# Modulation products of a transformer program as streamed TensorE matmuls in four column strips

## The reference

```python
cond = jax.nn.silu(c)
for l in range(DEPTH):
    mod = cond @ ada_w[l] + ada_b[l]          # [1024] @ [1024, 6144], DEPTH = 2
    sh1, sc1, g1, sh2, sc2, g2 = [m[:, None, :] for m in jnp.split(mod, 6, axis=-1)]
    h = _rms_norm(x, norm_mix[l]) * (1.0 + sc1) + sh1
    y = _even_mixer(h, ...) if l % 2 == 0 else _odd_mixer(h, ...)
    x = x + g1 * (y @ w_out[l])
    h = _rms_norm(x, norm_ffn[l]) * (1.0 + sc2) + sh2
    x = x + g2 * _swiglu(h, ffn_gate[l], ffn_up[l], ffn_down[l])
```

## Time and profile before

| | |
|---|---|
| median of three runs | 3065.33 us (3062.31 to 3065.77) |
| the profiled execution | 3062.31 us; its span is 3062.3 us, nothing lies around it |
| busy: PE, DVE, ACT, POOL | 91%, 46%, 35%, 35% of the span |
| mean granted TensorE clock | 0.918 of full speed |
| loads | 264.5 MB, DMA engines 27% busy |

### The profile page before, as it was taken

One profiled execution on the slowest core, in us unless ns is written; L12 is line 12 of the kernel. 1 busy time (PEld: TensorE's weight loads), 2 busy tenths in 40 slices (PEclk: granted clock), 3 DMA queues, 4 the chain that ended last, 5 costly groups with the idle time before them and its releaser, 6 DMA issues.

```text
span 3062.3 us, 34663 instructions
## 1 busy us (share of the span) xinstructions
PE 2800.6 (91%) x12655; PEld 2262.4 (74%) x12655; DVE 1417.1 (46%) x2167; ACT 1071.9 (35%) x1745; POOL 1077.0 (35%) x535
## 2 busy tenths in 40 slices
PE   4985689999999988999999999999999999799998
PEld 3764357777787667888878888888888765588886
DVE  6489872455412784222123566523331279533312
ACT  2221432322323474333223555523332322433321
POOL 1321000344443223444423565544444321144442
PEclk6897656999999999999988999999999999899998
DMA  7431040355433101223221221123322221122231
GB/s 215 138 110 55 1 138 14 97 164 164 137 100 85 63 28 56 83 82 110 94 74 55 69 69 56 56 83 100 105 91 92 86 63 41 42 96 96 96 97 55
DMA packets 277694, 264.50 MB, mean 86 GB/s; under 512 B 23020, under 2 KB 276557, under 8 KB 277581
## 3 DMA queue, kind: packets, MB, share of 16 engines
q1 hardware_dynamic: 277581, 262.97, 27.0%
HBM read 260.85 MB, written 2.10 MB: 86 GB/s over the span
## 4 chain that ended last, share of the span: by engine, by line
PE 71%; DVE 14%; issue 7%; DMA 3%; ACT 2%; POOL 2%; SPq 1%; DVEq 0%; ACTq 0%; POOLq 0%
PE bank L1151 17%; PE bank L1153 16%; PE bank L1152 16%; DMA root<-in_ada_w_dram 2%; DVE ada_acc L2392 2%; POOL w_lo L809 2%; PE bank L1099 1%; PE bank L883 1%; PE bank L885 1%; PE bank L884 1%; DVE bank L2216 1%; PE bank L1509 1%; DVE root L2398 1%; PE bank L1440 1%; DVE score L2575 1%
## 5 line engine op out<-in xcount | busy, mean ns | idle before, releaser
L809 POOL TENSOR_TENSOR w_lo<-w_raw,w_hi 128x1024 fp32r<-128x1024 f32 (+1 forms) x364 | 865.6, 2387 | 1674.2 <-ACT w_hi L1758 1103.3
L1151 PE MATMUL bank<-h_hi,w_hi 128*128 128x512 f32 x1632 | 651.6, 399 | 25.8 <-DVE h_lo L2359 11.6
L1152 PE MATMUL bank<-h_lo,w_hi 128*128 128x512 f32 x1632 | 645.4, 395 | 0.0
L1153 PE MATMUL bank<-h_hi,w_lo 128*128 128x512 f32 x1632 | 644.6, 395 | 0.0
L1758 ACT ACTIVATE w_hi<-w_raw 128x1024 fp32r<-128x1024 f32 (+1 forms) x232 | 232.2, 1014 | 510.7 <-PE bank L1153 438.9
L1151 PEld LDWEIGHTS bank<-h_hi,w_hi 128*128 128x128 f32 x1632 | 312.7, 192 | 95.7 <-issue 25.0
L1152 PEld LDWEIGHTS bank<-h_lo,w_hi 128*128 128x128 f32 x1632 | 313.1, 192 | 66.3 <-issue 1.7
L1153 PEld LDWEIGHTS bank<-h_hi,w_lo 128*128 128x128 f32 x1632 | 312.3, 191 | 66.5
L1153 PE MATMUL bank<-a_hi,w_lo 128*128 128x512 f32 x704 | 274.2, 389 | 0.0
L1151 PE MATMUL bank<-a_hi,w_hi 128*128 128x512 f32 x704 | 274.2, 389 | 0.0
L1152 PE MATMUL bank<-a_lo,w_hi 128*128 128x512 f32 x704 | 274.2, 389 | 0.0
(11 more groups left out here) (352 smaller groups left out, 4671.3 us busy)
## 6 DMA issues: line engine op xcount, KB each, us to landing
ada_w<-in_ada_w_dram SPq DMA_DIRECT2D x60, 512.0 KB, 6.1
w_raw<-in_ffn_gate_dram SPq DMA_DIRECT2D x22, 1024.0 KB, 5.2
w_raw<-in_ffn_up_dram SPq DMA_DIRECT2D x22, 1024.0 KB, 5.2
w_raw<-in_ffn_w_gate_dram SPq DMA_DIRECT2D x22, 1024.0 KB, 5.1
w_raw<-in_ffn_w_up_dram SPq DMA_DIRECT2D x22, 1024.0 KB, 5.1
root<-in_ada_w_dram SPq DMA_DIRECT2D x144, 128.0 KB, 2.4
w_raw<-in_ffn_down_dram SPq DMA_DIRECT2D x16, 1024.0 KB, 5.1
w_raw<-in_ssm_w_in_dram SPq DMA_DIRECT2D x16, 1024.0 KB, 5.2
```

Of the source, the lines that this page charges most:

```text
L809: pool.tensor_tensor(w_lo[parity][:, 0:nk, half], w_raw[parity][:, 0:nk, half], w_hi[parity][:, 0:nk, half].bitcast(F32), ALU.subtract).th ...
L1151: pe.matmul(dst[m][:], hi, src_hi(k0 + k), start=first and k == 0, stop=False)
L1152: pe.matmul(dst[m][:], hi, src_lo(k0 + k), start=False, stop=False)
L1153: ins = pe.matmul(dst[m][:], lo, src_hi(k0 + k), start=False, stop=last and k == nk - 1)
```

## The change

A group's product becomes matmuls. The stationary operand is a column of `cond`, repeated 32 times, the moving operand a 128 x 256 piece of `ada_w`; the pieces k = j and k = 4+j go to partitions 32j to 32j+31 of `bank[7]`, so a half of a group (512 KB, four pieces) is four matmuls in four column strips (`ada_rows`). Two groups make a block of 512 outputs; 24 blocks in all. When a block's four halves are done, ACT (DVE in the start) copies the bank to `ada_row`, four small matmuls with `ada_pick` (a one in rows 0, 32, 64, 96) add the strips and turn them into columns (`ada_columns`), and DVE adds the bias (`ada_add`). All of it goes through `bank[7]`, so one block must be added before the next begins.

Blocks 0 to 3 are at the start, 4 to 9 in the projections (rows after odd slots, columns after even ones), 10 to 23 in the two attentions: over steps k = 0 to 41 counted through both (19 steps of the first), two halves, two halves, then the columns. The first gate and up loop has none, and its loads of `ada_w` are gone. Two more buffers join the ring; in the attentions a ring of four is used. ACT now finishes the first norm's root before it rounds the first two weight slots.

```diff
-ADA_FIRST, ADA_PROJ, ADA_EVEN, ADA_ALL = 8, 21, 30, 48
-ADA_PER_STEP = 2
+ADA_BLOCKS, ADA_FIRST, ADA_PROJ = 24, 4, 10
 ADA_RING = 6
-N_CONSTS = 15
+N_CONSTS = 20
...
-        ada_w = [in_big(f"ada_w{j}", [P, 4, SLOT_W], 46 + 4 * j if j < 2 else 72 + 4 * (j - 2)) for j in range(ADA_RING)]
-        ada_acc = [in_big(f"ada_acc{j}", [P, SLOT_W], 54 + j) for j in range(2)]
+        ada_at = [46, 50, 72, 76, 80, 84, 24, 28]
+        ada_w = [in_big(f"ada_w{j}", [P, 4, SLOT_W], ada_at[j]) for j in range(ADA_RING + 2)]
+        ada_row = in_big("ada_row", [P, 2 * SLOT_W], 54)
...
-            hg = 2 * g + half
-            if g >= ADA_PROJ:
-                return half, 2 * ADA_PROJ // ADA_RING + g - ADA_PROJ
-            return hg % ADA_RING, hg // ADA_RING
+            if g < 2 * ADA_PROJ:
+                return (2 * g + half) % ADA_RING, (2 * g + half) // ADA_RING
+            late = 2 * g + half - 4 * ADA_PROJ
+            if late % 4 < 2:
+                before = len([q for q in range(4 * ADA_PROJ) if q % ADA_RING == late % 4])
+                return late % 4, before + late // 4
+            return ADA_RING + late % 4 - 2, late // 4
...
                 for half in range(2):
                     buf, _ = ada_half(g, half)
-                    if g >= ADA_PROJ:
-                        last = g - 1 if g > ADA_PROJ else ADA_PROJ - ADA_RING // 2
-                        sp.wait_ge(ada_dve, 8 * last + 4 * half + 4)
-                    elif g >= ADA_RING // 2:
-                        sp.wait_ge(ada_dve, 8 * (g - 3) + 4 * half + 4)
+                    late = 2 * g + half - 4 * ADA_PROJ
+                    if late >= 4:
+                        sp.wait_ge(ada_used, 2 * g + half - 4 + 1)
+                    elif late >= 2:
+                        sp.wait_ge(idx_summed, len(idx_units))
+                    elif late >= 0:
+                        sp.wait_ge(ada_used, max(q for q in range(4 * ADA_PROJ) if q % ADA_RING == late) + 1)
+                    elif 2 * g + half >= ADA_RING:
+                        sp.wait_ge(ada_used, 2 * g + half - ADA_RING + 1)
                     src = t["ada_w"][l, 512 * half:512 * half + 512, c0:c0 + SLOT_W]
...
-                def pieces(i, j):
-
-                    first = SLOT_W * (ADA_EVEN - ADA_ALL // 2 - 2 * ADA_PER_STEP)
-                    for q in range(8 * j, 8 * j + 8):
-                        t_, k = divmod(q, 8)
-                        sp.wait_ge(ada_dve, i * 16 + (8 * ADA_EVEN - 32 - 3 + q))
-                        src = t["ada_w"][1, P * k:P * k + P, bass.ds(i * (ADA_PER_STEP * SLOT_W) + (first + SLOT_W * t_), SLOT_W)]
-                        sp.dma_start(ada_piece[q % 4], src).then_inc(ada_piece_in[q % 4], 16)
-
-                def gate_up(i, with_ada):
+                def gate_up(i):
 
                     for j, w in enumerate((wg, wu)):
                         sp.wait_ge(w_split, i * 4 + 2 * (n0 + j - 1))
                         sp.dma_start(w_raw[(n0 + j) % 2][:], w.rearrange("(k p) m -> p k m", p=P)[
                             :, :, bass.ds(i * SLOT_W, SLOT_W)]).then_inc(w_full[(n0 + j) % 2], 16)
-                        if with_ada:
-                            pieces(i, j)
-
-                if f == 0:
-                    for i in range(2):
-                        gate_up(i, False)
-                    sp.wait_ge(h_ready, H_BASE[1] + DC)
-                    with sp.Fori(2, FC // 2) as i:
-                        gate_up(i, True)
-                else:
-                    with sp.Fori(0, FC // 2) as i:
-                        gate_up(i, False)
+
+                with sp.Fori(0, FC // 2) as i:
+                    gate_up(i)
...
-            for g in range(3):
+            for g in range(5):
                 load_ada(g)
             for n in range(2):
                 load_slot(n, even[n])
-            for g in range(3, ADA_FIRST):
+            for g in range(5, 2 * ADA_FIRST):
                 load_ada(g)
             even += [[(0, t["w_out"][0][:, 256 * m:256 * m + 256])] for m in range(4)]
             for n in range(N_EVEN):
                 load_slot(n + 2, even[n + 2])
                 if n == 0:
                     later_loads()
-                load_ada(ADA_FIRST + n)
-            for g in range(ADA_PROJ - 1, ADA_EVEN):
+                load_ada(2 * ADA_FIRST + n)
+            for g in range(2 * ADA_PROJ, 2 * ADA_BLOCKS):
                 load_ada(g)
...
-            ada_at = [0]
-
-            def ada_sums(upto_group):
-
-                for g in range(ada_at[0], upto_group):
-                    if g == 8:
-                        pe.wait_ge(gains_ready, 1)
-                    pe.wait_ge(ada_dve, 8 * g + 8)
-                    for j in range(2):
-                        ins = pe.matmul(bank[7][:, 2 * g + j:2 * g + j + 1], ada_acc[g % 2][:, P * j:P * j + P], ones[:, 0:1],
-                                        start=True, stop=True)
-                    ins.then_inc(ada_col, 1)
-                ada_at[0] = max(ada_at[0], upto_group)
+            def ada_rows(g, half):
+
+                buf, uses = ada_half(g, half)
+                if g % 2 == 0 and half == 0:
+                    take(7, ada_copied, g // 2 + 1)
+                    if g >= 2:
+                        pe.wait_ge(ada_added, g // 2)
+                pe.wait_ge(ada_full[buf], 16 * (uses + 1))
+                at = SLOT_W * (g % 2)
+                for j in range(4):
+                    ins = pe.matmul(bank[7][32 * j:32 * j + 32, at:at + SLOT_W],
+                                    cond[:, 4 * half + j:4 * half + j + 1].to_broadcast([P, 32]), ada_w[buf][:, j, :],
+                                    start=half == 0, stop=half == 1)
+                ins.then_inc(ada_used, 1)
+
+            def ada_columns(b):
+
+                pe.wait_ge(ada_copied, b + 1)
+                for j in range(4):
+                    ins = pe.matmul(bank[7][:, j:j + 1], ada_row[:, P * j:P * j + P], ada_pick[:], start=True, stop=True)
+                ins.then_inc(ada_col, 1)
+
+            def ada_block(b):
+                for g in (2 * b, 2 * b + 1):
+                    for half in range(2):
+                        ada_rows(g, half)
 
 
...
-            ada_sums(ADA_FIRST - 1)
-            norm_sums(0)
-            ada_sums(ADA_FIRST)
-            spread(0)
+            pe.wait_ge(cond_ready, 1)
+            for b in range(ADA_FIRST):
+                if b == 2:
+                    norm_sums(0)
+                ada_block(b)
+                if b == 2:
+                    spread(0)
+                ada_columns(b)
...
             def after_even(s):
-                ada_sums(ADA_FIRST + s)
+                if s % 2 == 1:
+                    ada_block(ADA_FIRST + s // 2)
+                elif s >= 2:
+                    ada_columns(ADA_FIRST + s // 2 - 1)
...
+            def ada_late(k):
+
+                b, part = divmod(k, 3)
+                if b < ADA_BLOCKS - ADA_PROJ:
+                    b += ADA_PROJ
+                    if part < 2:
+                        for half in range(2):
+                            ada_rows(2 * b + part, half)
+                    else:
+                        ada_columns(b)
...
+            def ada_copy(b):
+
+                act.wait_ge(ada_used, 4 * b + 4)
+                act.wait_ge(ada_col, b)
+                act.activation(ada_row[:], bank[7][:], ACT.Copy).then_inc(ada_copied, 1)
...
+            norm_squares(0)
+            rms("n0", (x_sq_summed, 1), D, NORM_EPS[0])
             round_slots(-2, 2)
-            norm_squares(0)
             norm(0)
...
+            def ada_add(b):
+
+                dve.wait_ge(ada_col, b + 1)
+                dve.tensor_tensor(mod[:, 4 * b:4 * b + 4], bank[7][:, 0:4], col_range("ada_b", 4 * b, 4), ALU.add
+                                  ).then_inc(ada_added, 1)
...
-                if f == 0:
-                    with dve.Fori(0, FC // 2 - 2) as i:
-                        gate_up(i)
-                        late_ada(i)
-                    with dve.Fori(FC // 2 - 2, FC // 2) as i:
-                        gate_up(i)
...
+                with dve.Fori(0, FC // 2) as i:
+                    gate_up(i)
...
-            for g in range(ADA_FIRST):
-                ada_group(g)
-                if 1 <= g < DC - 1:
-                    add_squares(0, g, g + 1)
+            add_squares(0, 1, DC - 1)
+            for b in range(ADA_FIRST):
+                if b == 2:
+                    rinv_recip(0)
+                ada_copy(b)
+                ada_add(b)
```

More of the change, by code:

```diff
@@ L1399, in swiglu, with attention @@
                     freed[b] = (x_ready, x0 + 5 + b)
-            def attention(name, scores, blocks, values, npair, nyb, u0, heads, waits=(), ring=3, back=7, ada=None):
+            def attention(name, scores, blocks, values, npair, nyb, u0, heads, waits=(), ring=3, back=7, ada_step=None):
                 for w in waits:
@@ L1456, in attention @@
                         do_scores(step)
```

(2 more changed lines are left out.)

145 lines of the change are left out of this document (60 added, 85 removed).

## The result

The changed kernel takes 3047.35 us (median of 4, 3039.12 to 3048.38); the kernel before, in the same comparison, 3064.34 (3062.31 to 3065.77). The ratio is 0.9936, with a 95% interval of 0.9922 to 0.9950: faster, by 17 us or 0.6%. The forecast was 3043. The profiled execution took 3046.64, its span is 3044.7.

The account below looks back on a forecast made before the run. Limits by stage: DVE's products in the start, PE then DVE in the projections, a dependency chain in the first attention, PE in the second. Terms -9 - 20 + 29 + 39 - 35 gave 3066, less 23 for clock: 3043 us, range 2985 to 3155.

Parts of the forecast that it names:

- the likeliest case: Whole kernel: strips side by side, part of the attentions at full clock, 3043 us (3020 to 3058), chance 0.42.
- Strips side by side: All blocks: four column strips run at once, a half costing 0.86 to 1.0 us cold, 0.44 to 0.55 warm.
- Projections, -20: Projections: DVE loses eight product groups after 175 us, PE gains three blocks at +9 before; -20 us.
- the loop, -35: First gate and up loop: without DVE's products, waits and column sums it becomes the second loop, -35 us.
- Start, -9: Start: DVE's products replaced by blocks at half-clock prices, `norm(0)` at 53 instead of 61.9 us.
- Attentions, +68 less 23 for the clock: Both attentions: +29 first and +39 second for strips and columns, -23 for a higher clock.
- The term for the columns with their wait: Attentions: 2.5 us a time, six times, in the first; 1.7 and 1.1 of waiting, eight times, in the second.
- A third of the attentions at full clock: Attentions: strips raise the clock for a third of 264 us, 88 us, saving 23 us.
- case 2: Attentions: strips side by side but the clock stays at 0.50; 3066 us (3056 to 3080), chance 0.18.
- A clock that is up throughout a stage: Attentions: strips raise the clock nearly throughout, -76 us; 2990 us (2975 to 3015), chance 0.15.
- Case 4: All blocks: a half's four strips run one after another; 3154 us, up to 3240, chance 0.20.
- The wait beyond its price: Attentions: single bank and copy behind the exponential cost 5 us, 14 times; 3085 us (3070 to 3110), chance 0.05.

Follow-up runs that it names:

- full_columns: Changed kernel with each strip product taking all 128 array columns, so a half's four pieces stand in a row: 3120.7 us, ratio 1.0182.
- no_proj: Changed kernel without the six blocks of the projections and their loads: 3043.7 us, ratio 0.9936.
- act_order: Changed kernel with ACT again rounding the first two weight slots before the first norm's squares and root: 3061.6 us, ratio 0.9989.
- no_late: Changed kernel with blocks 10 to 23 left out on all engines, loads included: 2967.3 us, ratio 0.9686.
- rows_only: Changed kernel keeping the strips of blocks 10 to 23 but without their copies, column matmuls, additions and PE's waits for them: 2972.7 us, ratio 0.9705.
- wait_only: Changed kernel keeping strips, ACT's copy and PE's wait for it, without column matmuls and additions of blocks 10 to 23: 3013.2 us, ratio 0.9831.
- rows_twice: rows_only with each half's four strips in the attentions issued twice: 2965.3 us, ratio 0.9696.
- both_first: copy_first with DVE's addition for a block also moved to the head of its step: 2990.1 us, ratio 0.9745.
- warm_strips: both_first with 8 extra strips in each of 28 steps, overwritten by the real ones: 2991.7 us, ratio 0.9761.
- both_mid: both_first with PE's strips and columns right behind the scores of their step, not behind its values: 3005.6 us, ratio 0.9825.
- copy_first: Changed kernel with ACT's copy for the columns moved ahead of the exponential of its step: 3001.1 us, ratio 0.9795.

## Why the prediction was right

The sign, the size and the likeliest case held. The number owes something to luck: the start came out 7 us cheaper than its term and the attentions 7 us dearer, and within the attentions larger errors cancelled. Point by point:

- **Strips side by side.** Right. A half takes 0.93 cold and 0.48 warm, forecast 0.86 to 1.0 and 0.44 to 0.55 from a neighbour, two products on row halves. full_columns shows what hung on it: 73 us and the sign.
- **Projections, -20, and the loop, -35.** Both right to the microsecond. DVE's chain still sets 175 to 267 us, and no_proj shows that the blocks there cost DVE nothing; all six cost 8 us, where the sum had 9 for the first three. The first loop is now as long as the second.
- **Start, -9; measured -15.9.** Mis-sized: half-clock prices were taken for a stretch that ran at 0.80. The remark that ACT's earlier root costs nothing was true and missed the point. The sum began the blocks at 23 us because the squares ran at 17.8, and act_order shows that this order alone is worth 21 us there.
- **Attentions, +68 less 23 for the clock; measured +52.** The sum was near, its terms were not. The forecast had 45 for strips, 37 for columns, -23 for the clock, and -14 for DVE's products and column sums removed. From the profiled executions: no_late against before is -21, strips with the clock that came with them +1 (rows_only), the wait +42 (wait_only), and columns with additions +30, which makes +52. The term for the columns with their wait was half of what they cost, 37 against 72: the hole was 1.7 us a time, not 0.6 to 1.3, and with it the last eight units ran at 0.50. Those units are 17 us of the strips' +1 and of the wait's +42; without them strips are +18 and the wait is +25.
- **The clock.** "A third of the attentions at full clock" did not come. From the clocks of the table, 0.72 and 0.55, some 61 of 257 us were at full clock, and 27 of 204 before, an estimate: 34 us more and not 88. With strips and no waits (rows_only) the second attention ran at 0.77.
- **Rivals.** The second attention stayed near half clock as in case 2, yet the total was not its 3066, since the start was 7 and the attentions 16 us cheaper than in its sum. A clock that is up throughout a stage came only in rows_twice, with no columns and twice the strips, and there only in the second attention, 0.98. Case 4 was priced too high: full_columns is at 3121, with 12 us in the start, 19 in the projections and 48 in the attentions where it has 29, 15 and 67 or more (its dearest terms add up to 3244, not 3240). The wait beyond its price, given 0.05, is what came: 72 us over 14 times is 5.1, where that case has 5. It was the largest error of the sum, made up for by strips and clock, which together came out 21 us cheaper.

The fastest version that leaves nothing out is both_first: 2990.1 us, ratio 0.9745 (0.9718 to 0.9771), four times the gain of the change as made. warm_strips, at 2991.7, cannot be told from it.

## What to carry to other kernels

Compare two traces stretch by stretch, and above all a stretch that the edit left alone, before giving a difference to the edit. By total time 47 us of strips cost 5 and 25 us of holes cost 40; where they stand, they cost 18 and 25, and the rest was the last eight units, the same instructions at full or at half clock. So take the step out and look at the stage's clock as well as its length, and remove waits first, above all a copy placed behind work that it does not need. When a program moves a load or a product earlier, look at what else on the in-order engine stood behind it: here the order of squares and rounding on ACT carried most of the net gain.

## What the runs showed of the hardware

Four matmuls of 32 columns over all 128 rows run side by side: eight of 256 float32 columns took 1.00 us to the next start at full clock, against 3.45 for eight that take all columns. The granted clock was not a matter of how busy TensorE was. It was 0.51 with 101 of 106 us busy on scores, turnings and values (no_late) and 0.54 with 135 of 139 busy (both_mid), but 0.98 with 90 of 96 busy (rows_twice), when eight strips a half stood between them in two of three steps. Nor was it a matter of the instructions that ran: the last eight units took 43.0 us at 0.50 with PE busy throughout (wait_only and eight other kernels), and 26.1 us at 1.00 with PE busy for 24.0 (rows_only, rows_twice and copy_first). What in both_mid kept the clock down, with fewer holes than in copy_first, stays open, and so do what decides the clock of the last eight units and the scatter within one kernel: both_first ran from 2977.0 us at a mean clock of 0.947 to 2998.1 at 0.939.
